# Indexer scores of the decode sequences: eight sequences in one PSUM bank by 32-column groups, instead of one after the other

## What is computed

```
s     = einsum('bqhd,bsd->bqhs', qi, ki)            # 16 heads x 2049 keys, each sequence
score = einsum('bqh,bqhs->bqs', wi, relu(s))        # one weight per head, summed over heads
idx   = top_k(score, 256)                           # keys that the attention then gathers
```

## Time and profile before

| what | value |
|---|---|
| device time, three runs | 2267.82, 2275.55, 2278.88 us; median 2275.55 |
| profiled execution, first to last instruction (span) | 2270.9 us |
| PE busy, share of the span | 2187.1 us, 96% |
| DVE, ACT, POOL busy | 1253.7, 509.4, 757.5 us |
| mean granted TensorE clock | 0.988 of full speed |

### The profile page before, as it was taken

One profiled execution on the slowest core, in us unless ns is written; L12 is line 12 of the kernel. 1 busy time (PEld: TensorE's weight loads), 2 busy tenths in 40 slices (PEclk: granted clock), 3 DMA queues, 4 the chain that ended last, 5 costly groups with the idle time before them and its releaser, 6 DMA issues.

```text
span 2270.9 us, 35542 instructions
## 1 busy us (share of the span) xinstructions
PE 2187.1 (96%) x15142; PEld 1886.4 (83%) x15158; DVE 1253.7 (55%) x1492; ACT 509.4 (22%) x649; POOL 757.5 (33%) x254
## 2 busy tenths in 40 slices
PE   7999999999999999999999999999999989999997
PEld 1225999966678898899899999999988889997776
DVE  2113666644467788787755667777853371113333
ACT  2112122233322212222212121221221131122222
POOL 0003333333323323323243433444445433333331
PEclk9999999999999999999999999999999999999999
DMA  9875322333242222232243323334445543333222
GB/s 348 290 259 177 88 79 74 88 101 91 61 131 78 70 81 81 65 83 78 71 114 94 81 72 100 83 83 107 110 138 174 159 139 93 92 94 131 93 93 113
DMA packets 324655, 258.55 MB, mean 114 GB/s; under 512 B 6245, under 2 KB 274721, under 8 KB 323241
## 3 DMA queue, kind: packets, MB, share of 16 engines
q1 hardware_dynamic: 312547, 228.09, 34.2%
q0 software_dynamic: 5120, 16.77, 2.5%
q10 hardware_dynamic: 6912, 12.59, 1.7%
HBM read 246.42 MB, written 11.48 MB: 114 GB/s over the span
## 4 chain that ended last, share of the span: by engine, by line
PE 83%; DVE 11%; issue 2%; ACT 2%; DMA 1%; SPq 1%; POOL 0%; DVEq 0%; ACTq 0%
PE acc L1309 57%; PE ps L1666 7%; PE acc L1321 6%; DVE ebuf L1025 2%; DVE qiT L900 2%; PE ps L1378 1%; PE ps L1422 1%; PE ps L1430 1%; PE acc L1666 1%; DVE ebuf L1026 1%; DMA ring<-in_w_ada 1%; PE ps L1493 1%; PE ps L1503 1%; PE ps L1415 1%; PE ps L1483 1%
## 5 line engine op out<-in xcount | busy, mean ns | idle before, releaser
L430 POOL TENSOR_TENSOR wlo<-raw,whi 128x2048 fp32r<-128x2048 f32 (+1 forms) x170 | 683.2, 4023 | 1142.8 <-ACT whi L527 959.0
L1309 PE MATMUL acc<-act_hi,whi 128*128 128x260 f32 x3904 | 814.5, 290 | 10.4 <-DVE act_lo L1153 6.2
L1309 PE MATMUL acc<-act_hi,wlo 128*128 128x260 f32 x3904 | 790.3, 284 | 0.0
L1309 PE MATMUL acc<-act_lo,whi 128*128 128x260 f32 x3904 | 790.3, 284 | 0.0
L1309 PEld LDWEIGHTS acc<-act_hi,whi 128*128 128x128 f32 x3904 | 610.0, 190 | 31.1 <-issue 21.3
L1309 PEld LDWEIGHTS acc<-act_lo,whi 128*128 128x128 f32 x3904 | 607.1, 190 | 0.0
L1309 PEld LDWEIGHTS acc<-act_hi,wlo 128*128 128x128 f32 x3904 | 606.6, 190 | 0.0
L527 ACT CAST whi<-raw 128x2048 fp32r<-128x2048 f32 (+1 forms) x154 | 280.9, 1824 | 1023.3 <-PE acc L1309 863.1
L1321 PE MATMUL acc<-ring,misc 128*9 128x512 f32 x384 | 168.6, 596 | 7.5 <-DVE misc L826 3.8
L1321 PEld LDWEIGHTS acc<-ring,misc 128*9 128x9 f32 x384 | 33.9, 91 | 132.1 <-issue 120.9
L900 DVE TENSOR_TENSOR qiT<-qiT,swp 128x520 f32<-128x520 f32 x32 | 142.7, 4458 | 1.1
(11 more groups left out here) (262 smaller groups left out, 2223.1 us busy)
## 6 DMA issues: line engine op xcount, KB each, us to landing
raw<-in_w_in SPq DMA_DIRECT2D x106, 1024.0 KB
ring<-in_w_ada SPq DMA_DIRECT2D x48, 1024.0 KB, 5.1
raw<-in_w_a_proj SPq DMA_DIRECT2D x16, 1024.0 KB
raw<-in_w_out SPq DMA_DIRECT2D x16, 1024.0 KB
raw<-in_w_b_proj SPq DMA_DIRECT2D x16, 512.0 KB
x_tok<-in_x_prompt SPq DMA_DIRECT2D x4, 1024.0 KB, 17.0
att_dram<-silu_ga ACTq DMA_DIRECT2D x16, 256.0 KB, 2.6
ksel<-out_k_s ACTq DMA_DIRECT2D x16, 256.0 KB, 5.4
```

Of the source, the lines that this page charges most:

```text
L430: return nc.gpsimd.tensor_tensor(wlo[p][:, a:b], raw[p][:, a:b], whi[p][:, a:b].bitcast(F32), ALU.subtract)
L1309: last = mm(acc[p][:, a, 0:HALF], w, x[:, k, a * HALF:(a + 1) * HALF], start=(k == 0 and n == 0), stop=(k == kt - 1 and n == 2))
```

## The change

Four sequences are handled at a time, each with 32 columns of the array, that is 32 partitions of PSUM. `round_scores(k)` takes four chunks (kept in four `kiTc` buffers instead of two) and writes their scores to partitions 0, 32, 64 and 96 of bank `ps[3]`. Two rounds fill a block: the stationary operand of a sequence is 32 wide, with its 16 heads in the lower or the upper half and zeros in the other, and round 1 adds to round 0. Then one Relu of 128x512 and one product with a 128x8 weight matrix (`wiD`, now in `misc`) do a whole block of eight sequences. That matrix is made much earlier: one small PE product copies the head weights to all 128 partitions (`eye8`), and DVE multiplies it with a table `own8`, which is one more small DMA at the start. `qiS` and `eye8` are set up by DVE behind the modulation.

```
-        def chunk_relu(u, n=512):
-            act.wait_ge(S("si_qk"), u + 1)
-            if u >= 2:
-                act.wait_ge(S("si_hr"), u - 1)
-            nc.scalar.activation(reluS[u % 2][:, 0:n], ps[0:HEADS, 3, 0:n], ACT.Relu).then_inc(S("si_relu"), 1)
+        def block_relu(n, width=512):
+            act.wait_ge(S("si_qk"), 2 * n + 2 if n < 4 else 9)
+            if n:
+                act.wait_ge(S("si_hr"), n)
+            nc.scalar.activation(reluS[:, 0:width], ps[:, 3, 0:width], ACT.Relu).then_inc(S("si_relu"), 1)
...
-            if u >= 2:
-                act.wait_ge(S("si_qk"), u - 1)
-            nc.scalar.copy(kiTc[u % 2][:].rearrange("p (c r) -> p r c", r=4),
+            if u >= 4:
+                act.wait_ge(S("si_qk"), u // 4)
+            nc.scalar.copy(kiTc[u % 4][:].rearrange("p (c r) -> p r c", r=4),
...
+                         (own8, t["k_own"]))):
...
+        dve.wait_ge(S("act_lo_ready"), KT)
+        step(v.memset(qiS[:], 0.0))
+        step(v.tensor_copy(eye8[:].rearrange("h (a b) -> h a b", b=HEADS),
+                           ident[0:HEADS, 0:HEADS].unsqueeze(1).broadcast_to([HEADS, NB, HEADS])))
...
+        v.tensor_tensor(wiD, ps[:, 3, 48:56], own8, ALU.mult).then_inc(S("wiD_ready"), 1)
...
-                step(v.memset(wiD[:], 0.0))
-                v.tensor_copy(wiD[:].rearrange("h a b -> h (a b)")[:, 0:64:9], wiT[:, SEQ:TOK]).then_inc(S("wiD_ready"), 1)
...
+        mm(ps[:, 3, 48:56], eye8[:], wiT[:, SEQ:TOK], start=True, stop=True)
...
-        def chunk_score(u):
-            pe.wait_ge(S("si_ka"), u + 1)
-            if u:
-                pe.wait_ge(S("si_relu"), u)
-            mm(ps[0:HEADS, 3, :], qiS[:, u % NB, :], kiTc[u % 2][:], start=True, stop=True).then_inc(S("si_qk"), 1)
-
-        def chunk_sum(u):
-
-            n, b = divmod(u, NB)
-            pe.wait_ge(S("si_relu"), u + 1)
-            if b == 0 and n:
+        def round_scores(k):
+
+            n, r = divmod(k, 2)
+            pe.wait_ge(S("si_ka"), 4 * k + 4)
+            if r == 0 and n:
+                pe.wait_ge(S("si_relu"), n)
+            for j in range(4):
+                last = mm(ps[32 * j:32 * j + 32, 3, :], qiS[:, 128 * r + 32 * j:128 * r + 32 * j + 32], kiTc[j][:],
+                          start=(r == 0), stop=(r == 1))
+            last.then_inc(S("si_qk"), 1)
+
+        def block_sum(n, width=512):
+
+            pe.wait_ge(S("si_relu"), n + 1)
+            if n:
                 pe.wait_ge(S("si_q"), n)
-            mm(ps[0:NB, 1, :], wiD[:, b, :], reluS[u % 2][:], start=(b == 0), stop=(b == NB - 1)
-               ).then_inc(S("si_hr"), 1)
+            mm(ps[0:NB, 1, 0:width], wiD, reluS[:, 0:width], start=True, stop=True).then_inc(S("si_hr"), 1)
...
-            if u >= 2:
-                chunk_sum(u - 2)
-            if 1 <= u <= CHUNKS:
-                chunk_score(u - 1)
+            if u and u % 4 == 0:
+                round_scores(u // 4 - 1)
+            if u > 8 and u % 8 == 1:
+                block_sum(u // 8 - 1)
             if u < CHUNKS:
                 chunk_transpose(u)
```

More of the change, by code:

```diff
@@ L134, in build @@
     qSm = at("qSm", A0 + 2816, [P, NB, KVH, HEADS])
-    qiS = at("qiS", A0 + 4864, [P, NB, HEADS])
     sgaS = at("sgaS", A0 + 5376, [P, HEADS, NB])
@@ L178, in build @@
     kib = [at(f"kib{s}", BG + 2048 * s, [P, 4 * P]) for s in range(3)]
-    kiTc = [at(f"kiTc{s}", A3 + 19552 + 2048 * s, [P, 512]) for s in range(2)]
-    reluS = [at(f"reluS{s}", A3 + 23648 + 2048 * s, [HEADS, 512]) for s in range(2)]
-    wiD = at("wiD", A3 + 27744, [HEADS, NB, NB])
+    kiTc = [at(f"kiTc{s}", A3 + 19552 + 2048 * s, [P, 512]) for s in range(4)]
+    reluS = at("reluS", A3 + 30912, [P, 512])
+    qiS = at("qiS", A3 + 71232, [P, 288])
+    eye8 = at("eye8", A3 + 72384, [HEADS, P])
     pgi = at("pgi", 0, [P, NB, PAGES], I32)
@@ L245, in build @@
     rcnt = misc[:, 152:216]
+    own8 = misc[:, 216:224]
+    wiD = misc[:, 224:232]
     sel8 = misc[0:16, 414:478]
@@ L251, in build @@
     lane = misc[:, 403:404]
+    qiS_rows = qiS[:].rearrange("p (r x) -> p r x", x=144)[:, :, 0:P].rearrange("p r (j c) -> p r j c", c=32)
     vS = misc[:, 480:512].rearrange("p (k b) -> p k b", b=NB)
@@ L312, in _ @@
                          (sel8, t["k_sel"]),
-                         (rcnt, t["k_rcnt"]), (tri[:], t["k_tri"]), (lane, t["k_lane"]))):
+                         (rcnt, t["k_rcnt"]), (tri[:], t["k_tri"]), (lane, t["k_lane"]),
+                         (own8, t["k_own"]))):
             sp.dma_start(dst, src).then_inc(S("tables_landed"), 16)
@@ L468, in _ @@
         pool.wait_ge(S("kv_evac"), 8)
-        pool.wait_ge(S("si_hr"), CHUNKS + 1)
+        pool.wait_ge(S("si_hr"), 5)
         value_head(0)
@@ L533, in root @@
                                  scale=1.0 / D).then_inc(S("root_ready"), 1)
-        act.wait_ge(S("tables_landed"), 10 * 16)
+        act.wait_ge(S("tables_landed"), 11 * 16)
         nc.scalar.copy(identb[:], ident[:]).then_inc(S("identb_ready"), 1)
@@ L613, in chunk_keys @@
             act.wait_ge(S("si_T"), u + 1)
-            if u >= 2:
-                act.wait_ge(S("si_qk"), u - 1)
-            nc.scalar.copy(kiTc[u % 2][:].rearrange("p (c r) -> p r c", r=4),
+            if u >= 4:
+                act.wait_ge(S("si_qk"), u // 4)
+            nc.scalar.copy(kiTc[u % 4][:].rearrange("p (c r) -> p r c", r=4),
                            ps[:, 2, :].rearrange("p (r c) -> p r c", r=4)).then_inc(S("si_ka"), 1)
-        def chunk_relu(u, n=512):
-            act.wait_ge(S("si_qk"), u + 1)
-            if u >= 2:
-                act.wait_ge(S("si_hr"), u - 1)
-            nc.scalar.activation(reluS[u % 2][:, 0:n], ps[0:HEADS, 3, 0:n], ACT.Relu).then_inc(S("si_relu"), 1)
+        def block_relu(n, width=512):
[3 more added lines that the diff above has]
+            nc.scalar.activation(reluS[:, 0:width], ps[:, 3, 0:width], ACT.Relu).then_inc(S("si_relu"), 1)
         def chunks_of_tile(j):
             for u in range(4 * j - 4, 4 * j):
-                if u:
-                    chunk_relu(u - 1)
+                if u and u % NB == 0:
+                    block_relu(u // NB - 1)
                 chunk_keys(u)
@@ L637, in _ @@
         chunks_of_tile(8)
-        chunk_relu(CHUNKS - 1)
-        chunk_relu(CHUNKS, n=NB)
+        block_relu(3)
+        block_relu(4, width=1)
         def body_c(h, first=False):
@@ L813, in _ @@
         dve.wait_ge(S("pages_landed"), 16)
-        dve.wait_ge(S("tables_landed"), 10 * 16)
+        dve.wait_ge(S("tables_landed"), 11 * 16)
         for i in range(4):
@@ L927, in index_query @@
             rope(Q_A + 1 + i, p, N_A + 1 + i, qiT[p][:], S("qi_ready"), h + 1)
-            v.tensor_copy(qiS[:, :, bass.ds(h, 1)], qiT[p][:, SEQ:TOK].unsqueeze(2)).then_inc(S("qiS_done"), 1)
+            v.tensor_copy(qiS_rows[:, :, :, bass.ds(h, 1)],
+                          qiT[p][:, SEQ:TOK].rearrange("p (r j) -> p r j", j=4).unsqueeze(3)).then_inc(S("qiS_done"), 1)
         index_query(0, 0, first=True)
@@ L958, in sample_quarter @@
         def sample_quarter(n):
-            dve.wait_ge(S("si_hr"), 8 * n + 8)
+            dve.wait_ge(S("si_hr"), n + 1)
             v.tensor_copy(scoreS[:, 512 * n:512 * n + 512], ps[0:NB, 1, :]).then_inc(S("si_q"), 1)
@@ L992, in _ @@
         v.tensor_copy(stok[:, 1, :], ps[0:NB, 2, :]).then_inc(S("stok_ready"), 1)
-        dve.wait_ge(S("si_hr"), CHUNKS + 1)
+        dve.wait_ge(S("si_hr"), 5)
         step(v.tensor_copy(scoreS[:, PAST:PAST + 1], ps[0:NB, 1, 0:1]))
@@ L1326, in _ @@
         tr = nc.tensor.transpose
-        pe.wait_ge(S("tables_landed"), 10 * 16)
+        pe.wait_ge(S("tables_landed"), 11 * 16)
         tr(ps[:, 0, 0:128], rows_cs[:], ident[:])
@@ L1456, in _ @@
         chunk_stages(CHUNKS + 1)
[L1458 to L1461, removed]
+        pe.wait_ge(S("si_relu"), 4)
+        for r in range(2):
+            for j in range(4):
+                last = mm(ps[32 * j:32 * j + 32, 3, 0:1], qiS[:, 128 * r + 32 * j:128 * r + 32 * j + 32],
+                          kiT[:, SEQ + 4 * r + j:SEQ + 4 * r + j + 1], start=(r == 0), stop=(r == 1))
         last.then_inc(S("si_qk"), 1)
@@ L1469, in _ @@
         last.then_inc(S("stok_T"), 1)
[L1470 to L1474, removed]
+        block_sum(4, width=1)
         pe.wait_ge(S("stok_ready"), 1)
@@ L1706, in shape_constants @@
         "k_rcnt": np.ascontiguousarray(np.broadcast_to((1.0 / cnt).astype(np.float32).reshape(1, 64), (P, 64))),
+        "k_own": np.array([[float(r // 32 == b % 4 and r % 32 // 16 == b // 4) for b in range(NB)] for r in range(P)],
+                          np.float32),
         "k_lane": (np.arange(P) % 32).astype(np.float32).reshape(P, 1),
```

## The result

The changed kernel takes 2209.33 us (median of four runs, 2207.69 to 2210.99); the kernel before, run beside it, 2277.22 (2267.82 to 2279.32). The ratio is 0.9712, 95% interval 0.9696 to 0.9728: faster by some 66 us (67.9 between the medians), where 43.8 were forecast. A second set of runs on another occasion gave 0.9748 [0.9725, 0.9771]: 2214.43 (2211.75 to 2216.78, five runs) beside 2272.52. The forecast of 2231.8 and its range down to 2218 lie above both. The profiled execution has a span of 2205.8 us, 65.1 less than before's, and took 2207.69, 1.9 above its span; its mean clock is 0.992.

The account below looks back on a forecast made before the run. PE was taken as the bound, busy 96% of the span. Gain 61.1 + 6.2 - 3.8 - 18.1 - 0.9 - 0.5 - 0.2 = 43.8 us, so 2275.55 - 43.8 = 2231.8 us; range 2218 to 2246.

Parts of the forecast that it names:

- the added rounds: Score work on PE: eight rounds of four two-pass products cost 18.1 us, with 7.7 and 28.5 as ends.
- this middle value: Score rounds on PE: passes start in order, neighbouring groups share one slot, 2.26 us a round; chance 0.45.
- the lower one: Lower bound for a score round: four column groups side by side, 0.96 us, time 2221.4; rival's chance 0.22.
- Removed sums and scores: Chunk stages on PE: 32 sums and scores go, at 0.95 + 0.96 us each, saving 61.1 us.
- the wait at chunk 0: Before chunk 0's transposes: PE's 4.94 us wait and the slow patch behind it go, together 6.2 us.
- four sums at 0.95: Block sums on PE: four added 128x512 products by eight columns cost 0.95 us each, 3.8 us.
- no fall of the clock in the tiles: Tiles with rounds: granted clock stays 1.00; the rival, a fall to 1.2 GHz costing 9.6 us a tile, had 0.03.
- DVE's work fits: Tiles with a round: DVE's 12.2 us of work fits in the shortened tile of 17.0 us.
- The tail: From chunk 31's transposes to the next tile: 6.38 + R, adding 0.9 us.
- R: Time of one round of four score products on PE: taken as 2.26 us, between 0.96 and 3.56.
- The start's small costs: Set-up: one more table DMA, taken as 0.5 us, and the `eye8` product, 0.2 us at most.
- The gathers' margin of 3.3 us: Gathers land 13.7 us behind transposes, wanted after 17.0, leaving 3.3; a later-gather rival (2253) had chance 0.03.

Follow-up runs that it names:

- e3: The changed kernel, but each block's second round issues eight score products, two in a row on each column group; 2218.19 us, ratio 0.9768.
- e7: The changed kernel with one more 128x512 product by eight columns, read by nothing, in 15 stages holding transposes alone; 2228.73 us, ratio 0.9811.
- e2: The kernel before, with `wiD` at its own place and filled right behind `wiT`, nothing else changed; 2263.92 us, ratio 0.9979.
- e4: The changed kernel with a fourth `kib` gather buffer and the last value head's transposes ahead of the last round; 2205.17 us, ratio 0.9722.
- e6: The changed kernel with a fourth gather buffer and earlier last value transposes, run a second time; 2207.25 us, ratio 0.9716.
- e5: The changed kernel as it is, run a second time; 2214.43 us, ratio 0.9748 against the kernel before.

## Why the prediction was wrong

**The step that failed** is that on the added rounds: "If starts stay in order, the second pass of group j and the first pass of group j+1 can share a slot and no more [...] I take this middle value." The round takes 1.00, not 2.26; eight rounds (the last 1.06) cost 8.0 us, not 18.1. The bounds were right and the lower one was nearly true: 0.96 was worked out. The reason against it, that no row gave a sign of passes overtaking each other, was no evidence, since no row could have shown it: every product of the trace wrote from partition 0. Of the two sentences of the Trainium skill named there ("TensorE: Matmul & The Clock Gate", section "Part 3: Packing small matmuls — row/col tiling"), the span model agrees with the trace within a few ns (starts 7 ns apart where it gives about 4), and the strict program order does not hold between groups for these two-pass products (e3).

**A term that was missing.** Twenty plain stages have no narrow product ahead of their transposes any more: 20 x 0.15 = 3.0 us of gain. The forecast counted sum and score from start to start, and left what stands beside them as it was. e7 shows that this changes too.

**Terms that held.** Removed sums and scores 61.1; the wait at chunk 0 6.2 (e2: 6.45, its whole gain in the stretch); four sums at 0.95; no fall of the clock in the tiles; DVE's work fits. The tail is 6.98 where 6.38 + R with the true R is 7.38, 0.4 better. The start's small costs can't be judged: 0.58 us were lost for 0.7 forecast, but e2, which has none of them, lost 0.43, and the change's second run 1.84 (there with a granted clock of 0.91 from 180 to 200 us, 1.00 in the first). Only a step of 0.21 at the place of the `eye8` product shows, for 0.2.

**A cost that was called nil.** The gathers' margin of 3.3 us was worked out for chunks a full tile apart. Chunk 3 is wanted less than a tile behind chunk 0, at 463.17. Its gather reuses chunk 0's buffer, so it is written behind POOL's first `wlo` row: chunk 0's transposes are done by 453.7, but that row runs from 453.53 to 458.15, the gather goes out at 458.30, and PE waits 1.10. The other margins held, in tiles down to 14.82 us. With the 1.86 us wait of the second query tile (0.58 in before) the change thus gives some of its time to waits that e4 and e6 take back. Before's row of that wait:

```profile
651.45 0.51 PE L1309 MATMUL acc<-act_hi,whi 128*128 128x260 f32 x2 [0.58 <-POOL wlo L430]
```

**The sum as it came out**, for the stretch: 61.1 + 6.2 - 3.8 - 8.0 + 3.0 - 1.1 - 0.5 = 56.9 us, for 57.1 measured (-0.5 is the tail's 0.9 less 0.4). The forecast's terms for the stretch made 44.5, so it was 12.6 short, and 10.1 of that is the round. With the true round the forecast would have read 2221.7 us, still 12.4 above the measured median of the first set and 7.3 above that of the second; the rest is the 2.5 us of the other terms and what lies outside the stretch.

**What lies beside it.** The medians differ by 67.9 us in the first set of runs and 58.1 in the second. The 57.1 less the start's 0.6 is 56.5; what goes beyond it moves with where the clock falls and with that one wait in the sample attention. The 1.4 us of the tile behind the stretch were there in all seven profiles of the change and its variants, and the forecast has no term for them. How much of the rest, if any, is the change's lasting effect on the clock in the heads stays open: two profiles of it differ by 5.8 us at their ends, nearly all outside the stretch.

## What to carry to other kernels

Small products that write to different 32-partition groups of a bank run side by side, also in float32 with its two passes: here four cost what one costs (1.00 us, 0.96), and their written order among groups mattered little (e3). Where a price hangs on an overlap that no row can show, the absence of a sign in the trace is no argument for the middle of the bounds; give the ends their full weight. When work is taken out from between other work, price what stands beside it too (0.15 us a stage here), and look at the first and last tile of the stretch for transfers that the removed time used to cover.

## What the runs showed of the hardware that was not expected

- Passes of one group follow each other 0.43 us apart, those of the four groups start 7 ns apart in the change and 13 ns apart in e3; a group runs ahead of products written before its own.
- A 512-wide product of 8 columns between the tile's products and four 128x128 transposes costs 1.10 us, 0.95 of its own and 0.15 beside it; by the chain the transposes then take 0.59 us instead of 0.44 (e7 turns the one into the other).
- Behind one and the same wait of 2.9 us the granted clock fell in some executions and not in others (0.79 and 0.89 against 1.00 and 1.00), worth 1.5 us for the tile behind e5's wait. What decides it, no run here tells.
- In the tile right behind the stretch the granted clock over 12 us is 0.87 in both profiles with before's code ahead of it and 1.00 in all seven with the change's, worth 1.4 us. Why, no run here tells.
